# Twenty-four tokens off the expert stream instead of sixteen, their x copied to all partitions by GpSimd, in a one-core transformer layer

## The reference, cut to what matters

```
qry = (t @ wq); s = qry . sub_keys            # 8 heads, 2 x 128 keys
top 16 of each side, then top 16 of the 256 sums -> 128 experts for each token
gate = softmax(top_s)
a   = gelu(einsum('ted,td->te', down[expert], t))     # 128 dot products of 1024 for each token
out = einsum('te,ted->td', a * gate, up[expert])
```

## Time and profile before

| what | value |
|---|---|
| runs | 1058.26, 1066.93, 1061.05 us, median 1061.05 |
| profiled execution | 1059.69 us, span of its instructions 1057.9 us |
| granted TensorE clock, mean | 0.992 |
| PE, PEld, DVE, ACT, POOL busy | 97%, 86%, 75%, 51%, 10% |
| down tiles | from 294.07 to 679.7 us of the span |
| up tiles | from 679.7 to 1050.6 us |

### The profile page before, as it was taken

How to read it: one execution, slowest core, us unless ns; L and a number is a source line. 1 busy time by engine, 2 the same in 40 slices (tenths; PEclk the granted TensorE clock), 3 DMA queues, 4 the chain that set the end, 5 groups by cost and what they waited for, 6 DMA issues and landing times.

```text
span 1057.9 us, 18483 instructions
## 1 busy us (share of the span) xinstructions
PE 1028.5 (97%) x7388; PEld 912.5 (86%) x7388; DVE 797.0 (75%) x1434; ACT 535.8 (51%) x870; POOL 103.4 (10%) x86
## 2 busy tenths in 40 slices
PE   8999999999999789999999999999999999999996
PEld 8988888898799789979999999988888888888885
DVE  5667767857599987567989988798889885555575
ACT  5564544554465436566555555444444445545551
POOL 3000000000079400112221000000000000000000
PEclk9999999999999989999999999999999999999999
DMA  9943334733346536788888555655555556656671
GB/s 319 384 143 100 101 121 159 248 128 102 116 156 196 178 120 197 243 301 292 300 282 291 172 177 182 208 186 178 173 169 178 167 172 197 188 193 198 189 249 40
DMA packets 56373, 203.44 MB, mean 192 GB/s; under 512 B 6480, under 2 KB 6528, under 8 KB 55904
## 3 DMA queue, kind: packets, MB, share of 16 engines
q1 hardware_dynamic: 49824, 178.80, 51.9%
q0 software_dynamic: 6464, 23.46, 6.3%
HBM read 200.60 MB, written 1.11 MB: 191 GB/s over the span
## 4 chain that ended last, share of the span: by engine, by line
PE 85%; DVE 9%; DMA 3%; ACT 1%; issue 1%; SPq 0%; DVEq 0%
PE psS L1890 16%; PE psT L1890 16%; PE psG L1502 12%; PE psG L1503 11%; PE psG L1504 11%; PE psG L1835 4%; DMA raw<-in_down 2%; PE psG L1837 2%; PE psO L1858 1%; PE psO L1859 1%; DVE unit_c L1150 1%; DMA raw<-in_w_stream 1%; PE psT L1876 1%; PE psO L1782 1%; PE psS L1504 1%; PE psS L1502 1%
## 5 line engine op out<-in xcount | busy, mean ns | idle before, releaser
L730 ACT ACTIVATE hi<-raw 128x1024 fp32r<-128x1024 f32 x325 | 343.5, 1059 | 293.3 <-DMA raw<-in_up 180.4
L975 DVE TENSOR_TENSOR lo<-raw,hi 128x1024 fp32r<-128x1024 f32 x301 | 366.5, 1221 | 93.7 <-ACT hi L730 92.7
L1502 PE MATMUL psG<-b_two,hi 128*128 128x240 f32 (+1 forms) x848 | 238.4, 281 | 12.2 <-DVE lo L975 10.4
L1504 PE MATMUL psG<-b_two,lo 128*128 128x240 f32 (+1 forms) x848 | 234.5, 277 | 0.0
L1503 PE MATMUL psG<-b_two,hi 128*128 128x240 f32 (+1 forms) x848 | 234.5, 276 | 0.0
L1502 PEld LDWEIGHTS psG<-b_two,hi 128*128 128x128 f32 x848 | 161.3, 190 | 14.7 <-DVE lo L975 10.6
L1503 PEld LDWEIGHTS psG<-b_two,hi 128*128 128x128 f32 x848 | 161.4, 190 | 0.1
L1504 PEld LDWEIGHTS psG<-b_two,lo 128*128 128x128 f32 x848 | 161.2, 190 | 0.0
L1480 DVE TENSOR_TENSOR act_lo<-H,act_hi 128x256 fp32r<-128x256 f32 x128 | 53.7, 423 | 89.4 <-ACT act_hi L954 89.4
L1835 PE MATMUL psG<-b_two,hi 128*128 128x480 f32 x240 | 80.4, 386 | 2.6 <-DVE H L1425 2.6
L1890 PE MATMUL psS<-hi,act_hi 128*128 128x512 f32 x240 | 77.0, 402 | 0.0
(11 more groups left out here) (370 smaller groups left out, 1817.7 us busy)
## 6 DMA issues: line engine op xcount, KB each, us to landing
raw<-in_down SPq DMA_DIRECT2D x128, 512.0 KB, 3.6
raw<-in_up SPq DMA_DIRECT2D x128, 512.0 KB, 3.5
raw<-in_w_stream SPq DMA_DIRECT2D x73, 512.0 KB, 3.6
x_all<-apart_x POOLq DMA_DIRECT2D x16, 512.0 KB
w<-in_w SPq DMA_DIRECT2D x4, 512.0 KB, 13.4
xT<-in_xT SPq DMA_DIRECT2D x4, 256.0 KB, 4.7
raw<-in_w_stream SPq DMA_DIRECT2D x4, 256.0 KB, 5.6
memT<-in_memT SPq DMA_DIRECT2D x1, 1024.0 KB, 7.0
```

Source lines behind the costliest of these rows:

```text
L730: act.activation(hi[hi_slot(n)][:], raw[slot(n)][:], ACT.Copy).then_inc(hi_done, 1)
L975: dve.tensor_tensor(lo[slot(n)][:], raw[slot(n)][:], hi[hi_slot(n)][:].bitcast(FP32), ALU.subtract)\
L1502: pe.matmul(out, hi_l, hi_r, start=start, stop=False)
L1504: return pe.matmul(out, lo_l, hi_r, start=False, stop=stop)
```

## The change

The number of tokens apart goes from 16 to 24, so the down matmuls have 232 columns instead of 240, and the gathers come every 2.5 tiles instead of every 3 (APART_AT), from tile 50 to tile 107. There are two row buffers instead of four and two x buffers instead of three. x of a token is no longer copied by a DMA from DRAM to all partitions: POOL issues a DMA of the one row (4 KB, SBUF to partition 0 of the x buffer), waits for it, and copies it to all partitions by `partition_broadcast`. WIDE is empty, all tiles take 24 matmuls. POOL makes lo of 34 down tiles instead of 24. DVE waits for PE's gates before it writes the one-hot factors of two more groups (30 and 62). At the start ACT issues the first weight tile in four quarters beside SP's x, and each quarter is split and waited for by itself; at the end ACT makes the last four activations before hi of tile 127.

```diff
--- before.py
+++ after.py
@@ -241,15 +241,15 @@
...
 ALL = N1 + 2 * E_TILES
-POOL_FROM, POOL_TO = N1, N1 + 24
+POOL_FROM, POOL_TO = N1, N1 + 34
 DECODE = 8
-WIDE = [j for j in range(48, 121) if j < HALF or j > 98 and j % 3]
-APART = 16
+WIDE = []
+APART = 24
 SD = S - APART
 APART_GROUP = SD // TOK
-APART_AT = [50 + 3 * k for k in range(APART)]
-APART_END = 98
-ROWS, X_ALL = 4, 3
+APART_AT = [50 + 5 * k // 2 for k in range(APART)]
+APART_END = 110
+ROWS, X_ALL = 2, 2
 ROWS_AT = E_TILES - 4 * (ROWS + X_ALL)
...
@@ -333,8 +333,10 @@
...
             g += 1
-        if j + 4 < E_TILES:
+        if j + 4 < E_TILES - 4:
             out.append(("act", j + 4))
+        if j == E_TILES - LAST:
+            out += [("act", E_TILES - 4 + i) for i in range(4)] + [("late", E_TILES - 1)]
     assert g == 2 * GROUPS
...
@@ -632,13 +634,10 @@
...
                 sp.dma_start(xT[:, part, :], a["xT"][:, part, :]).then_inc(x_in[i], 16)
-                if i % 2 == 0:
-                    half = slice(i * D // 4, (i + 2) * D // 4)
-                    sp.dma_start(raw[0][:, half], a["w_stream"][0][:, half]).then_inc(first_in[i // 2], 16)
             for n in range(1, FIRST):
...
                     half = slice(c * D // 2, (c + 1) * D // 2)
-                    sp.dma_start(raw[n][:, half], a["w_stream"][n][:, half]).then_inc(first_in[2 * n + c], 16)
+                    sp.dma_start(raw[n][:, half], a["w_stream"][n][:, half]).then_inc(first_in[4 + c], 16)
             for n in range(FIRST, ALL):
...
@@ -698,9 +697,7 @@
...
             pool.wait_ge(norm_ready, 2 * NT)
-            pool.dma_start(a["apart"], x2[P - APART:P, NT - 1, :]).then_inc(apart_x, 16)
             pool.wait_ge(expert_ready, 1)
-            pool.wait_ge(apart_x, 16)
             for k in range(APART):
...
@@ -708,11 +705,12 @@
...
                     .then_inc(rows_in[k % ROWS], 16)
-                pool.wait_ge(tile_used, DOWN + APART_AT[k] - 3)
                 if k >= X_ALL:
                     pool.wait_ge(products, k - X_ALL + 1)
-                pool.dma_start(x_all[k % X_ALL][:], a["apart"][k:k + 1, :].broadcast_to([P, D]))\
-                    .then_inc(x_all_in[k % X_ALL], 16)
+                row, first = P - APART + k, x_all[k % X_ALL][0:1, :]
+                pool.dma_start(first, x2[row:row + 1, NT - 1, :]).then_inc(x_row_in, 16)
+                pool.wait_ge(x_row_in, 16 * (k + 1))
+                pool.partition_broadcast(x_all[k % X_ALL][:], first).then_inc(x_all_in, 1)
 
...
@@ -820,18 +818,18 @@
...
             for i in range(4):
-                part = slice(2 * i, 2 * i + 2)
+                quarter = slice(i * D // 4, (i + 1) * D // 4)
+                act.dma_start(raw[0][:, quarter], a["w_stream"][0][:, quarter]).then_inc(first_in[i], 16)
+            for i in range(4):
+                part, quarter = slice(2 * i, 2 * i + 2), slice(i * D // 4, (i + 1) * D // 4)
                 act.wait_ge(x_in[i], 16)
                 act.activation(o_hi[:, part, :], xT[:, part, :], ACT.Copy).then_inc(split_hi, 1)
-                if i % 2 == 0:
-                    half = slice(i * D // 4, (i + 2) * D // 4)
-                    act.wait_ge(first_in[i // 2], 16)
-                    act.activation(hi[0][:, half], raw[0][:, half], ACT.Copy)\
-                        .then_inc((first_hi, hi_done)[i // 2], 1)
+                act.wait_ge(first_in[i], 16)
+                act.activation(hi[0][:, quarter], raw[0][:, quarter], ACT.Copy).then_inc(hi_done if i == 3 else first_hi, 1)
             for n in range(1, FIRST):
...
                     half = slice(c * D // 2, (c + 1) * D // 2)
-                    act.wait_ge(first_in[2 * n + c], 16)
+                    act.wait_ge(first_in[4 + c], 16)
                     act.activation(hi[n][:, half], raw[n][:, half], ACT.Copy).then_inc((first_hi, hi_done)[c], 1)
...
@@ -957,8 +955,8 @@
...
                         split(UP + late)
-                elif what == "last" and j == E_TILES - LAST:
-                    split(UP + E_TILES - 1)
+                elif what == "late":
+                    split(UP + j)
             for t in range(NT):
...
@@ -1112,15 +1110,14 @@
...
                     .then_inc(split_lo, 1)
-                if i % 2 == 0:
-                    half = slice(i * D // 4, (i + 2) * D // 4)
-                    dve.wait_ge((first_hi, hi_done)[i // 2], 1)
-                    dve.tensor_tensor(lo[0][:, half], raw[0][:, half], hi[0][:, half].bitcast(FP32), ALU.subtract)\
-                        .then_inc((first_lo, lo_done)[i // 2], 1)
+                quarter = slice(i * D // 4, (i + 1) * D // 4)
+                dve.wait_ge(hi_done if i == 3 else first_hi, 1 if i == 3 else i + 1)
+                dve.tensor_tensor(lo[0][:, quarter], raw[0][:, quarter], hi[0][:, quarter].bitcast(FP32), ALU.subtract)\
+                    .then_inc(lo_done if i == 3 else first_lo, 1)
             for n in range(1, FIRST):
...
                     half = slice(c * D // 2, (c + 1) * D // 2)
-                    dve.wait_ge((first_hi, hi_done)[c], n + 1)
+                    dve.wait_ge((first_hi, hi_done)[c], (4, 2)[c])
                     dve.tensor_tensor(lo[n][:, half], raw[n][:, half], hi[n][:, half].bitcast(FP32), ALU.subtract)\
...
@@ -1379,7 +1376,7 @@
...
                     dve.wait_ge(one_ready, g)
-                if g == GROUPS:
+                if g == GROUPS or g % GROUPS > APART_GROUP and g % 2 == 0:
                     dve.wait_ge(gates_done, g)
...
@@ -1426,7 +1423,7 @@
...
                 dve.wait_ge(rows_in[k % ROWS], 16 * (k // ROWS + 1))
-                dve.wait_ge(x_all_in[k % X_ALL], 16 * (k // X_ALL + 1))
+                dve.wait_ge(x_all_in, k + 1)
                 dve.tensor_tensor(rows[k % ROWS][:], rows[k % ROWS][:], x_all[k % X_ALL][:], ALU.mult).then_inc(products, 1)
...
@@ -1455,8 +1452,8 @@
...
                             rest(UP + late)
-                elif what == "last" and j == E_TILES - LAST:
-                    rest(UP + E_TILES - 1)
+                elif what == "late":
+                    rest(UP + j)
                 elif what == "decode":
...
@@ -1543,8 +1540,10 @@
...
                             pe.wait_ge(turn_lo, turned_in - 1 + k // 4)
-                        if n < FIRST and k % 4 == 0:
-                            pe.wait_ge((first_lo, lo_done)[k // 4], n + 1)
+                        if n == 0 and k % 2 == 0:
+                            pe.wait_ge(lo_done if k == 6 else first_lo, 1 if k == 6 else k // 2 + 1)
+                        if n == 1 and k % 4 == 0:
+                            pe.wait_ge((first_lo, lo_done)[k // 4], (4, 2)[k // 4])
                         if n == 0 and k % 2 == 0:
...
```

More of the change, by code:

```diff
@@ L556, in build @@
         x_in = [sem(f"x_in{i}") for i in range(4)]
-        first_in = [sem(f"first_in{i}") for i in range(2 * FIRST)]
+        first_in = [sem(f"first_in{i}") for i in range(4 + 2)]
         warm_ready = sem("warm_ready")
@@ L594, in build @@
         act_hi, act_lo = sem("act_hi"), sem("act_lo")
-        apart_x, expert_ready, products, dots_done, apart_gelu = (
-            sem("apart_x"), sem("expert_ready"), sem("products"), sem("dots_done"), sem("apart_gelu"))
+        expert_ready, products, dots_done, apart_gelu = (
+            sem("expert_ready"), sem("products"), sem("dots_done"), sem("apart_gelu"))
         rows_in = [sem(f"rows_in{i}") for i in range(ROWS)]
-        x_all_in = [sem(f"x_all_in{i}") for i in range(X_ALL)]
+        x_row_in, x_all_in = sem("x_row_in"), sem("x_all_in")
         dve_step, silu_ready = sem("dve_step"), sem("silu_ready")
@@ L1992 @@
            for k, v in arrays.items()}
-    aps["apart"] = nc.dram_tensor("apart_x", (APART, D), FP32, kind="Internal").ap()
     aps["out"] = nc.dram_tensor("out_x", (S, D), FP32, kind="ExternalOutput").ap()
```

## The result

The changed kernel took **1079.5 us** (median of 4 runs, 1076.4 to 1083.7) against 1061.0 (4 runs) of the kernel before: ratio 1.0172, 95% interval 1.0144 to 1.0200. I had forecast 1058, a little faster; it is slower by 1.7%. The profiled execution of after took 1076.38 us, its span 1074.6, so 16.7 us more than the profiled one of before, where I had summed up -2.8. My sum was off by 19.5 us.

What follows compares the result with a forecast made beforehand. PE, busy 97% of the span, was taken as the bound, with its waits. Terms -8.6 - 3.8 - 5.0 + 15.3 + 0.5 + 0.3 - 1.0 - 0.5 = -2.8 us gave 1056.9, forecast 1058; 8-in-10 range 1036 to 1082.

Steps and rivals of the forecast that it cites:

- Columns: Down tiles: 8 fewer columns take 0.084 us off each, to 2.604 us; -8.6 us in all.
- rival (c): Down tiles: narrower ones are no faster since weight loads pace them; +8.6 us, 1066.5; chance 0.05.
- The gathers: From tile 50 on: POOL's rounds are too long for 2.5 tiles, so PE waits 15.3 us in all.
- C: Length of POOL's round from gather through row DMA and broadcast: 8.0 us, low end 6.6, high end 9.7.
- their 0.5: Gates: one more group in each half takes three matmuls for a token instead of two; +0.5 us.
- The stall at tile 34: PE's wait moves from tile 24 to 34, 5.5 us plus 2.6 for half clock, against 13.1 before; -5.0 us.
- Wide waits: Wide tiles: PE's waits of 2.6 and 1.2 us for L1425 go; -3.8 us.
- End: Last tiles: PE's wait of 1.0 us for the activations goes; -1.0 us.
- Start: Kernel start: smaller first pieces save 0.5 of the 0.9 us PE waits for the first weight lo.
- The rival by which it is slower: Gathers: POOL's round is the bound by far, C = 9.2, PE waits 41.7 us; 1084 us; chance 0.23.
- Rival (a): Gathers: POOL's round fits 7.3 us, as row overtakes gather or broadcast nears memset; 1042.7 us; chance 0.33.
- broadcasts that stretch DVE's work: Gathers: a sign that would show the forecast wrong, broadcasts stretching DVE's products; no size given.

Runs made afterwards that it cites:

- widths: The kernel before with the down matmuls of single and wide tiles cut or widened to several column counts: single tiles of 232 to 128 columns all took 2.66 to 2.68 us.
- row_first: The changed kernel with the row DMA issued ahead of the gather instead of behind it: 1059.7 us, ratio 0.9982 to the kernel before.
- after_small: The changed kernel with the broadcast replaced by a memset of one column, row DMA still behind the gather: 1057.0 us, ratio 0.9955 to the kernel before.
- no_wide: The kernel before with WIDE empty, nothing else changed: 1058.1 us, ratio 0.9974.
- sixteen_late_decode: The changed kernel with 16 tokens apart, a gather every 3 tiles, and DVE's decodes at tiles 28 to 42 instead of 22 to 36: 1047.7 us, ratio 0.987.
- row_first_16_late: The changed kernel with 16 tokens at every third tile, row DMA ahead of the gather, and decodes six tiles later: 1046.8 us, ratio 0.9873.
- row_first_small: The changed kernel with the row DMA ahead of the gather and the broadcast replaced by a memset of one column: 1053.9 us, ratio 0.993.

## Why the prediction was wrong, step by step

Two terms make the 19.5 us by which the sum was off, about 10 us each. The gain of narrower tiles does not exist, which is an error of mechanism. The loss at the gathers was of the right mechanism and too small: POOL's round was taken too short, and the half clock behind PE's waits was put at nothing.

**Columns: -8.6 forecast, about +1 measured.** This is the step that failed in its mechanism: I took the time of a tile as going down with its columns, and from 232 down it does not. I drew a straight line through 256 and 240 columns and went on below. 98 tiles gained 0.0078 us each (-0.8, from stretches of four tiles) and the 30 formerly wide ones lost 2.68 - 2.62 (+1.8). It was rival (c), to which I gave 0.05 because the step from 256 to 240 seemed to speak against it; but that step lies wholly above the knee. The row that spoke for it was in front of me: single tiles took 2.69 us and wide ones of the same columns, with a third fewer weight loads, 2.62; I counted that as an advantage that goes and didn't ask what would pace a single tile if columns did not. The Trainium skill, TensorE: Matmul & The Clock Gate, section LDWEIGHTS (loading the stationary operand), gives a load of 128 columns as 128 / 1.2 = 106.7 ns, and its section Back-to-back issue gap says that load and matmul set the spacing together. The runs agree in kind: 111.7 ns, 5 above it, and no fall below. They do not agree with the 81 ns that the same section gives as sustained at 128 columns: in widths, with 4-byte data, it was 110.8 to 111.7 ns.

**The gathers: +15.3 forecast, and 26 us lost over their stretch.** The mechanism was right, with the row behind the gather and a broadcast of 1.44 us (1.5 taken). Mis-sized was C, 8.45 for 8.0, and each tenth of a microsecond counts 22 times. The trace's 21 rounds split it into 6.26 for the gather (5.9 taken), 0.43 until the row behind it (0.3), 1.40 for the broadcast and 0.36 for starts (0.3), so it is mostly the gather that was taken too short. With the measured values my own sum gives: the last broadcast ends at 21.2 + 22 x 8.45 = 207.1, its product is due at 19 x 2.68 + 47 x 2.97 - 4.9 = 185.6, difference 21.5; PE's idle time from tile 60 to 127 adds up to 18.7. What the sum lacked altogether is the clock: 6.8 us. I had priced it at tile 34 and nowhere else. Of the 26.0 us these two are 25.5; less the wait of 1.2 for L1425 that is gone, plus 18 wide tiles that lost their advantage (1.1), plus 0.2 of the gates (the other half of their 0.5 falls into the up tiles), less 0.4 that the single tiles gained, 25.2. So the loss is explained to within 1 us, and row_first and after_small each took most of it away by one edit. That is a sum of what PE lost, not of causes: the drops of the clock stand behind the waits, and most of the waits behind the round.

**The sum by stretches.** Forecast and measured shifts (us), the forecast's terms laid on the same tiles:

| | to tile 36 | 36 to 60 | 60 to 127 | end | sum |
|---|---|---|---|---|---|
| forecast | -8.5 | -3.8 | +10.5 | -1.0 | -2.8 |
| measured | -6.1 | -2.9 | +26.0 | -0.4 | +16.7 |

The columns make about 3, 2 and 5 us of the first three differences. In the second the wide tiles' waits gave back 1 us more than forecast, in the third the longer round and the clock make the remaining 10.

**The stall at tile 34: right, in its size partly by luck.** Forecast -5.0, measured -5.3 alone and -6.1 in the changed kernel. DVE's timeline of after, from the end of the searches to the lo of tile 34:

```profile
371.82 2.58 DVE L1333 TENSOR_TENSOR chosen_s<-chosen_s,gate_z 128x256 f32<-128x256 f32 x1
374.33 2.89 DVE L1335 CAST ranked_f<-ranked_i 128x1024 f16<-128x1024 uint32 x1
377.13 0.41 DVE L1338 CAST picked_f<-picked_ab 128x512 f16<-128x512 uint32 x1
377.58 3.31 DVE L1347 TENSOR_TENSOR picked_e<-iota,picked_f 128x2048 f16<-128x2048 f16 x1
380.93 3.31 DVE L1353 TENSOR_TENSOR picked_e<-picked_e,ranked_f 128x2048 f16<-128x2048 f16 x1
384.28 3.56 DVE L1359 TENSOR_TENSOR picked_e<-picked_e 128x1024 f16<-128x1024 f16 x3
...
394.71 2.35 DVE L973 TENSOR_TENSOR lo<-raw,hi 128x1024 fp32r<-128x1024 f32 x2
```

Of the same kind, before, with no lo of POOL beside them:

```profile
371.41 0.43 DVE L1336 TENSOR_TENSOR chosen_s<-chosen_s,gate_z 128x256 f32<-128x256 f32 x1
371.75 0.69 DVE L1338 CAST ranked_f<-ranked_i 128x1024 f16<-128x1024 uint32 x1
```

Five instructions were held by 2.15 + 2.20 + 2.09 + 2.08 + 2.09 = 10.6 us where I took 8 and bounded at 12. That made the lo ready at 395.9 instead of 393.0. PE came later too, at 391.5 for 387.5, since its tiles were no faster and tile 33 had waited 0.9 us for H. The two errors cancelled in the wait, 4.5 us for 5.5. The Trainium skill, SBUF — State Buffer, section SBUF: two separate sides, states just this rule: an exclusive lock of the shared ports that is held for the full instruction. The page that I cited in the prediction only says contention; this one gives the rule that I took from the rows, and these five agree with it. It also says that the DVE operations concerned have two SBUF inputs or a two-port mode; the cast with one input that took 2.89 us is at least not against the second.

**Wide waits: -3.8 forecast, -3.0 measured** (no_wide), net of 30 wide tiles that each lost 0.07, 2.1 in all. So their waits had cost about 5.1 us, more than the 3.8 that PE's list has: the step from tile 51 to 52, with a wait of 1.32, took 4.10 us where 2.61 and 1.32 make 3.93. **End:** the wait of 1.0 became 0.3, and the end's share is -0.4 for -1.0. **Start:** the first down tile began at +0.03 us, so the -0.5 did not come. The first weight matmul started 0.24 us sooner (6.12 for 6.36), but the second quarter then waited 1.1 us for its lo and started 0.53 later (8.23 for 7.70).

**The rival by which it is slower** named POOL's round as the bound and gave C = 9.2; the round was the bound with 8.45. My threshold, slower by over 1% from 8.65 (8.6 by its own terms), was passed sooner because the columns gave nothing and the clock took its part. **Rival (a)**, that the row overtakes the gather, is what row_first makes true by an edit; in the queue as written it never does. Of what I said would show me wrong, broadcasts that stretch DVE's work, half is true: in after the products all took 1.21 to 1.23 us, and what was stretched were one-hot rows (up to 1.57 us) and lo (up to 1.94). In row_first three of the 24 products were stretched as well, to 2.2 us, beside the broadcast into the other buffer.

## What to carry to other kernels

Where a loop of small transfers is paced by waits, multiply its round by its count and ask which transfer stands first in the queue: the small one that somebody waits for belongs ahead of the large one (19.8 us here by exchanging two blocks). Before trusting a slope of time over columns, ask for the floor beside it: two tile shapes with the same columns and different numbers of weight loads point to it, and one run with a few widths shows it. An engine that is idle is not free if its instructions lock out another that feeds the bottleneck; and a wait of PE is to be priced with the half clock that may follow it, at every place and not only at the largest.

## What the runs showed of the hardware

- Matmuls of 128 to 232 columns (4-byte data), each with its own load of 128x128 weights, start 111 to 112 ns apart; at 240 columns it is 112, at 248 115, at 256 119 to 120 (widths). Loads of 128x128 2-byte weights followed each other at 30 ns.
- A broadcast of a 4 KB row from one partition to 128 took 1.29 us, and up to 2.37 with a lo of DVE beside it (after, 578.95); beside broadcasts a one-hot product of DVE took up to 1.63 us for 0.69. The first broadcast of the kernel started 4.4 us after its row had landed (438.05 to 442.48), hidden here.
- A 4 KB transfer in POOL's queue landed 4.9 us after issue (median) behind a gather of 512 KB, in after and in sixteen_late_decode. Issued ahead of the gather it was 3.3 us in row_first_16_late (2.8 to 4.1) and 3.8 us in row_first_small.
- The instruction of POOL's indirect gather took 1.13 to 2.07 us directly behind a broadcast, 2.06 in half of the rounds (after), and 0.99 to 1.97, median 1.2, where the row DMA lay between (row_first). What lengthens it stays open.
